# First block: two projection units and four gate units as seven block products each, the sums of their weights on GpSimd

## What is computed

```python
h = rms_norm(x, pre_norm_g[l])
u = jnp.einsum('bsd,de->bse', h, w_in[l])
u_mla, u_sb, u_moba, u_conv, u_gate = jnp.split(u, SPLITS, axis=-1)
...
qb, kb, vb = jnp.split(u_sb, 3, axis=-1)
o_b = merge_heads(stick_breaking_attention(split_heads(qb, H), ...))
qc, kc, vc = jnp.split(u_moba, 3, axis=-1)
o_c = merge_heads(moba_attention(split_heads(qc, H), split_heads(kc, H), split_heads(vc, H), rel_bias))
o_d = conformer_conv(u_conv, ...)
y = jnp.concatenate([o_a, o_b, o_c, o_d], axis=-1) * jax.nn.silu(u_gate)
y = jnp.einsum('bse,ed->bsd', y, w_out[l])
x = x + rms_norm(y, post_norm_g[l])
```

## Time and profile before

| what | us |
|---|---|
| median of 3 runs | 1030.85 |
| lowest, highest | 1030.44, 1031.91 |
| the profiled execution, own time | 1033.43 |
| its span (first to last instruction) | 1031.6 |
| PE busy | 998.9 (97%) |
| DVE busy | 720.6 (70%) |
| ACT busy | 202.0 (20%) |
| POOL busy | 77.2 (7%) |
| mean granted TensorE clock | 0.992 of full |

### The profile page before, as it was taken

One profiled execution on the slowest core, in us unless ns is written; L12 is line 12 of the kernel. 1 busy time (PEld: TensorE's weight loads), 2 busy tenths in 40 slices (PEclk: granted clock), 3 DMA queues, 4 the chain that ended last, 5 costly groups with the idle time before them and its releaser, 6 DMA issues. The chain is left out here.

```text
span 1031.6 us, 14106 instructions
## 1 busy us (share of the span) xinstructions
PE 998.9 (97%) x5350; PEld 728.8 (71%) x5352; DVE 720.6 (70%) x1683; ACT 202.0 (20%) x488; POOL 77.2 (7%) x89
## 2 busy tenths in 40 slices
PE   7999999999999999999999999989999999999994
PEld 4858764858865799757777777658996677777762
DVE  2695654695644587656899888985874677766668
ACT  4124323115222221202000000022222110010000
POOL 2000000000000000000002000062850000000000
PEclk9999999999999999999999999999999999999998
DMA  9854556655465546383679877824453345654411
GB/s 353 350 194 176 187 180 253 257 200 205 151 216 218 210 170 239 91 318 120 207 253 355 292 256 264 282 93 164 144 186 122 123 163 168 225 179 164 163 41 41
DMA packets 29914, 205.56 MB, mean 199 GB/s; under 512 B 3630, under 2 KB 3795, under 8 KB 6172
## 3 DMA queue, kind: packets, MB, share of 16 engines
q1 hardware_dynamic: 27116, 191.60, 51.6%
q0 software_dynamic: 2736, 13.11, 3.5%
HBM read 203.64 MB, written 1.05 MB: 198 GB/s over the span
## 5 line engine op out<-in xcount | busy, mean ns | idle before, releaser
L1650 PE MATMUL bank<-hT,raw 128*128 128x256 f32 x736 | 163.9, 383 | 2.1 <-DMA raw<-units_dram 2.1
L1650 PEld LDWEIGHTS bank<-hT,raw 128*128 128x128 f32 x736 | 140.0, 192 | 23.1 <-DMA raw<-units_dram 2.8
L1939 PE MATMUL bank<-yT,arena 128*128 128x512 f32 x224 | 100.8, 593 | 0.0
L1939 PE MATMUL bank<-raw,arena 128*128 128x512 f32 x180 | 86.8, 593 | 0.0
L1939 PEld LDWEIGHTS bank<-yT,arena 128*128 128x128 f32 x224 | 42.5, 190 | 53.8 <-issue 51.7
L876 DVE CUSTOM_DVE_ANT_0 raw<-raw,crow 128x1024 f32<-128x1024 f32 x64 | 75.4, 1220 | 0.5 <-DVEq L118 0.5
L1963 PEld LDWEIGHTS bank<-hT,raw 128*128 128x128 f32 x448 | 54.3, 192 | 12.4 <-issue 12.4
L726 ACT ACTIVATE arena<-bank 128x512 f32<-128x512 f32 x28 | 16.7, 597 | 197.0 <-PE bank L1963 197.0
L1963 PE MATMUL bank<-hT,raw 128*128 128x128 f32 x448 | 54.5, 275 | 0.0
L1660 PE MATMUL bank<-raw,yT 128*128 128x512 f32 x112 | 49.5, 596 | 0.9 <-DVE yT L1544 0.4
L909 DVE SCALAR_TENSOR_TENSOR arena<-arena 128x256 f32<-128x256 f32 x120 | 48.4, 481 | 0.1
(11 more groups left out here) (427 smaller groups left out, 1710.4 us busy)
## 6 DMA issues: line engine op xcount, KB each, us to landing
raw<-units_dram SPq DMA_DIRECT2D x180, 1024.0 KB, 4.9
arena<-ln_rows_dram POOLq DMA_DIRECT2D x4, 1024.0 KB, 5.1
arena<-att_line_dram POOLq DMA_DIRECT2D x4, 512.0 KB, 6.4
arena<-small_dram POOLq DMA_DIRECT2D x2, 896.0 KB, 7.5
arena<-ada_rows_dram POOLq DMA_DIRECT2D x1, 1536.0 KB, 8.0
xt<-x_dram SPq DMA_DIRECT2D x2, 512.0 KB, 4.6
arena<-post_g_dram POOLq DMA_DIRECT2D x2, 512.0 KB, 9.3
kst<-consts_dram SPq DMA_DIRECT2D x1, 608.0 KB, 16.4
```

What stands on the lines that cost most here:

```text
L1650: mm = pe.matmul(b[:, c * S:(c + 1) * S], raw[:, s, k * 256 + c * P:k * 256 + (c + 1) * P], act_t[:, k, :], start=(k == 0), stop=(k == KC ...
L1939: return pe.matmul(SB[i][:], x, y, start=False, stop=stop)
```

## The change

A unit is the product of a 1024 x 256 weight matrix with 1024 x 256 tokens. Cut in 2 x 2 blocks (128 columns by 512 rows of weights, 512 rows by 128 tokens) it takes eight block products; by the scheme of Winograd and Strassen it takes seven, of sums of blocks, and more sums behind them. A block product is 4 matmuls of 128x128 weights against 128 tokens, so a unit becomes 28 matmuls of 128 columns where it was 16 of 256.

- `first_part` on PE: the first part of a unit is four products (two of plain blocks, two of sums), the rest is three. For `U_CQ` and `U_CK` the parts go to different banks, in the old place. For a gate unit both go to G[1] one after the other: the rest is multiplied after the head's transposes, next scores and values, and waits for `half_drained`; the next unit's first part waits for `first_drained` of the one before. The transposes of the queries now wait for `first_drained` of `U_CQ`, whose banks they use.
- `first_weights` on POOL: four tensor-tensor operations of 128x512 for each unit, from `raw` into `gateT`, `yT` or the place of `mu`, as soon as the unit has landed and its target is free.
- `first_token_sums` on DVE: four of 128x512 for a layer, `hT` into `xs`, between `taps(0, 12)` and `ada_unit(3)`.
- `half_sums` and `rest_sums` on DVE: seven small operations for each unit, from PSUM to `part`, `qkC` or `gateT`.
- ACT no longer drains the two units; it scales `qkC[:, 0]` in place. The tanh reads `gateT` and stands behind the copies and exponentials of the pair, and the gate product on DVE stands behind the normalisation (`gate`), except for the last.

```diff
+            def first_weights(l, u):
+                n = FIRST[u]
...
+                wait_landed(pool, T1 * l, n)
+                if u == 2:
+                    pool.wait_ge(up_ready.sem, up_ready.at(l, 2))
+                    pool.wait_ge(rope_ready.sem, rope_ready.at(l, 2))
+                if u >= 3:
+                    wait_used(pool, T1 * l, FIRST[(1, 2, 4)[u - 3]])
+                ch.do(pool.tensor_tensor(d[:, 0], a[1][0], a[1][1], ALU.add))
+                ch.do(pool.tensor_tensor(d[:, 2], a[0][0], a[1][0], ALU.subtract))
+                ch.sync(1)
+                ch.do(pool.tensor_tensor(d[:, 1], d[:, 0], a[0][0], ALU.subtract))
+                ch.sync()
+                pool.tensor_tensor(d[:, 3], a[0][1], d[:, 1], ALU.subtract).then_inc(fsum_ready.sem, 1)
...
+            def half_sums(l, u, b):
+                p, o = b[:].rearrange("p (i n) -> p i n", i=4), FIRST_OUT[u]
+                dve.wait_ge(first_half.sem, first_half.at(l, u + 1))
+                ch.do(dve.tensor_copy(part[:, 2], p[:, 0]))
+                ch.sync()
+                ch.do(dve.tensor_tensor(o[0][:, 0], part[:, 2], p[:, 1], ALU.add))
+                ch.do(dve.tensor_tensor(part[:, 0], part[:, 2], p[:, 2], ALU.add))
+                ch.sync()
+                dve.tensor_tensor(part[:, 1], part[:, 0], p[:, 3], ALU.add).then_inc(half_drained.sem, 1)
+            def rest_sums(l, u, b):
...
+                wait_used(dve, T1 * l, FIRST[u])
+                dve.wait_ge(half_drained.sem, half_drained.at(l, u + 1))
+                ch.do(dve.tensor_tensor(part[:, 2], part[:, 0], p[:, 1], ALU.add))
+                ch.do(dve.tensor_tensor(o[1], part[:, 1:2].to_broadcast([P, NT, P]), p[:, 0:2], ALU.add))
+                ch.sync(1)
+                ch.do(dve.tensor_tensor(o[0][:, 1], part[:, 2], p[:, 2], ALU.add))
+                ch.sync()
+                dve.sem_inc(first_drained.sem, 1)
...
                 taps(0, 12)
+                first_token_sums(l)
                 ada_unit(l, 3)
...
+                half_sums(l, 0, A[2])
+                rest_sums(l, 0, A[3])
+                half_sums(l, 1, G[0])
+                rest_sums(l, 1, G[1])
                 ada_unit(l, 5)
...
                     if j % 2 == 0:
-                        gate(j // 2)
+                        half_sums(l, 2 + j // 2, G[1])
...
                         if j + 2 < 2 * H:
                             scores_max(j + 2)
+                            ada_unit(l, 6 + j // 2)
+                            rest_sums(l, 2 + j // 2, G[1])
                             scores_max(j + 3)
                             head_norm(8 * l, j + 2)
                             head_norm(8 * l, j + 3)
-                        ada_unit(l, 6 + j // 2)
+                            gate(j // 2)
+                        else:
+                            rest_sums(l, 2 + j // 2, G[1])
+                            gate(j // 2)
+                            ada_unit(l, 6 + j // 2)
...
-                unit_t(T1 * l, U_CQ, hT, G[0])
-                unit_t(T1 * l, U_CK, hT, G[1])
+                pe.wait_ge(upc_ready.sem, upc_ready.at(l, 6))
+                for u, b in ((0, A[2:4]), (1, G[0:2])):
+                    for rest in range(2):
+                        first_part(l, u, b[rest], rest)
...
+                pe.wait_ge(first_drained.sem, first_drained.at(l, 1))
...
                     if j % 2 == 0:
-                        if j >= 2:
-                            pe.wait_ge(silu_ready.sem, silu_ready.at(l, j // 2))
-                        unit_t(T1 * l, U_GATE[j // 2], hT, G[1])
+                        pe.wait_ge(first_drained.sem, first_drained.at(l, 2 + j // 2))
+                        first_part(l, 2 + j // 2, G[1], False)
```

More of the change, by code:

```diff
@@ L245, in build @@
         zT = zline[:, 2:4, :]
+        part = rt.rearrange("p a t h i -> p (a t h i)")[:, 0:3 * P].rearrange("p (i n) -> p i n", i=3)
         view2 = views()
@@ L390, in build @@
         msum_ready, mtsum_ready, mix_drained = (sem(n) for n in ("msum_ready", "mtsum_ready", "mix_drained"))
+        FIRST = (U_CQ, U_CK) + U_GATE
+        square4 = lambda b: b.rearrange("p (i k n) -> p i k n", i=4, k=4)
+        first_tsum, f_gate, f_y = (square4(b[:].rearrange("p a b -> p (a b)")) for b in (xs, gateT, yT))
+        at_mu = NCOL + NSMALL + D + H * S
+        f_mu = square4(arena[:, at_mu:at_mu + UNIT])
+        FIRST_SUMS = (f_gate, f_y, f_mu, f_y, f_mu, f_mu)
+        FIRST_OUT = [[qkC[:, i, c].rearrange("p (t n) -> p t n", t=NT) for c in range(2)] for i in range(2)]
+        FIRST_OUT += [[gateT[:, 2 * g + c].rearrange("p (t n) -> p t n", t=NT) for c in range(2)] for g in range(H)]
+        ftsum_ready, fsum_ready, first_half = event("ftsum_ready", 1), event("fsum_ready", 6), event("first_half", 6)
+        half_drained, first_drained = event("half_drained", 6), event("first_drained", 6)
         def wait_landed(eng, turns, n):
@@ L456, in _ @@
             pool.dma_start(wgk[0:17, :], gk_in).then_inc(gla_in, 16)
+            def first_weights(l, u):
+                n = FIRST[u]
+                w = raw[:, n % SLOTS, :].rearrange("p (k n) -> p k n", k=KC)
+                a = [[w[:, 4 * k:4 * k + 4, c * P:(c + 1) * P] for k in range(2)] for c in range(2)]
+                d = FIRST_SUMS[u]
+                wait_landed(pool, T1 * l, n)
[10 more added lines that the diff above has]
+                pool.tensor_tensor(d[:, 3], a[0][1], d[:, 1], ALU.subtract).then_inc(fsum_ready.sem, 1)
             pool.wait_ge(rr_ready, 1)
@@ L464, in _ @@
             pool.tensor_copy(moba_bias[:], zline[:, :, ::-1]).then_inc(bias_ready, 1)
+            for u in range(6):
+                first_weights(0, u)
             for l in range(1, DEPTH):
                 layer_vectors(l)
+                for u in range(6):
+                    first_weights(l, u)
             pool.wait_ge(x_new.sem, 2 * DEPTH + 2)
@@ L646, in _ @@
                 act.activation(spl[:], spl[:], ACT.Ln, bias=1.0).then_inc(spl_ready.sem, 1)
-                wait_used(act, T1 * l, U_CQ)
-                act.activation(qkC[:, 0], G[0][:], ACT.Copy, scale=HD_SCALE).then_inc(qk_ready.sem, 1)
-                wait_used(act, T1 * l, U_CK)
-                act.activation(qkC[:, 1], G[1][:], ACT.Copy).then_inc(qk_ready.sem, 1)
+                act.wait_ge(first_drained.sem, first_drained.at(l, 1))
+                act.activation(qkC[:, 0], qkC[:, 0], ACT.Copy, scale=HD_SCALE).then_inc(qk_ready.sem, 1)
                 for i, (dst, h0, b) in enumerate(((qT, 0, A[2]), (qT, 2, A[3]), (kT, 0, A[1]), (kT, 2, A[2]))):
@@ L660, in gate_tanhs @@
                 def gate_tanhs(g):
-                    wait_used(act, T1 * l, U_GATE[g])
+                    act.wait_ge(first_drained.sem, first_drained.at(l, 3 + g))
                     if g >= 1:
                         act.wait_ge(silu_ready.sem, silu_ready.at(l, g))
-                    act.activation(th[:].rearrange("p c s -> p (c s)"), G[1][:], ACT.Tanh, scale=0.5).then_inc(gate_tanh.sem, 1)
+                    act.activation(th[:], gateT[:, 2 * g:2 * g + 2, :], ACT.Tanh, scale=0.5).then_inc(gate_tanh.sem, 1)
                 def head_scale(j):
@@ L1730, in last_units, with first_part, product @@
                             mm.then_inc(o_ready.sem, 1)
+            def first_part(l, u, b, rest):
+                n = FIRST[u]
+                w = raw[:, n % SLOTS, :].rearrange("p (k n) -> p k n", k=KC)
+                a, ts = FIRST_SUMS[u], first_tsum
+                def product(i, x, y):
+                    for k in range(4):
+                        mm = pe.matmul(b[:, i * P:(i + 1) * P], x(k), y(k), start=k == 0, stop=k == 3)
+                    return mm
+                if not rest:
+                    wait_landed(pe, T1 * l, n)
+                    product(0, lambda k: w[:, k, 0:P], lambda k: hT[:, k, 0:P])
+                    product(1, lambda k: w[:, 4 + k, 0:P], lambda k: hT[:, 4 + k, 0:P])
+                    pe.wait_ge(ftsum_ready.sem, ftsum_ready.at(l, 1))
+                    pe.wait_ge(fsum_ready.sem, fsum_ready.at(l, u + 1))
+                    product(2, lambda k: a[:, 1, k], lambda k: ts[:, 1, k])
+                    product(3, lambda k: a[:, 2, k], lambda k: ts[:, 2, k]).then_inc(first_half.sem, 1)
+                else:
+                    if u >= 2:
+                        pe.wait_ge(half_drained.sem, half_drained.at(l, u + 1))
+                    product(0, lambda k: w[:, 4 + k, P:S], lambda k: ts[:, 3, k])
+                    product(1, lambda k: a[:, 0, k], lambda k: ts[:, 0, k])
+                    product(2, lambda k: a[:, 3, k], lambda k: hT[:, 4 + k, P:S]).then_inc(used[n % SLOTS], 1)
             pe.wait_ge(zeros_ready, 1)
@@ L1809, in _ @@
                 pe.wait_ge(qkT_ready.sem, qkT_ready.at(l, 4))
[L1810 removed]
+                pe.wait_ge(qk_ready.sem, qk_ready.at(l, 3))
+                pe.wait_ge(first_drained.sem, first_drained.at(l, 2))
                 def head_scores(j):
```

(2 more changed lines are left out.)

19 lines of the change are left out of this document (15 added, 4 removed).

## The result

The changed kernel takes 1069.98 us (median of 4 runs, 1068.35 to 1070.88) beside 1031.38 (4 runs, 1030.44 to 1032.23) on the same chip: a ratio of 1.0375 [1.0359, 1.0391], 38.6 us slower. The forecast was 1075.0. The profiled execution took 1070.88; its span is 1069.0 against 1031.6 before, 37.4 more.

A forecast was written before the change was run, and what follows sets the result against it. PE was taken to bound the kernel, with DVE's slack ahead of the logarithms as the limit. Layers of 21.4 and 19.2 us plus 3.5 of clock made 44.1, on 1030.85 the forecast 1075.0, own range 1066 to 1086.

The forecast's parts named there:

- What bounds it: PE busy 97% of the span; DVE has only 3.11 us of slack ahead of the logarithms (5.29 in layer 1).
- PE's saving, 0.70 a unit: Seven-product units take 6.25 us for 6.95; 12 units save 8.4 us, 4.2 in a layer.
- Token sums, 2.4 us in the slack: Ahead of the logarithms, four DVE token sums of 0.6 us each fit in the 3.11 us of slack.
- POOL and DVE take turns, taps included: Ahead of the logarithms, three units' sums cost DVE 5.0 us each; transposes 13.4 us late in layer 0, 11.2 in layer 1.
- taps are free: Rival: in the first block only token sums and ada products lose turns, not the taps; 1051 us, chance 0.09.
- The range's other end: In the taps, up to 0.3 us more per turn as DVE restarts its pipe; 12 turns a layer, +7 us.
- Waits of the loop: In the gate loop, new PE waits less 0.7 saved per unit: net +3.0, +1.3, +0.65, +3.1 for `U_G0` to `U_G3`.
- The clock, 1.7 a layer: Behind PE's idle ahead of the transposes, the lower clock costs 1.7 us per layer, between 0 and 3.5; +3.5 in all.
- The sum: Whole kernel: 21.4 us in layer 0, 19.2 in layer 1, 3.5 of clock, 44.1 us in all.
- No turns at all, 2.75 a layer: Rival: no turns in the first block, 2.75 us slower per layer, 5.5 in all; 1036.4 us, chance 0.11.

The follow-up runs named there:

- experiment 1: The changed kernel with POOL's four weight sums per unit replaced by fills with zero of the same tiles; 1038.65 us, ratio 1.0066.
- experiment 4: The changed kernel with one wait more: POOL begins the first gate unit's sums only when ACT's softplus is ready; 1063.31 us, ratio 1.0307.
- experiment 6: The changed kernel with PE's wait for the last gate moved from ahead of the first output unit to ahead of the second; 1062.95 us, ratio 1.0316.
- experiment 8: The changed kernel with only the last three gates in seven products, and POOL's sums and DVE's ada units placed elsewhere; 1040.86 us, ratio 1.0092.
- experiment 2: The changed kernel with query and key units whole again, drained by ACT, only the gates in seven products; 1047.69 us, ratio 1.0165.
- experiment 9: The kernel of experiment 8 with POOL's sums of the third and fourth gates at other times only; 1033.26 us, ratio 1.0023.
- experiment 10: The kernel of experiment 9 with POOL's sums replaced by fills with zero; 1031.41 us, ratio 0.9999.
- experiment 3: The changed kernel with the gates whole again in their old order, only query and key units in seven products; 1048.60 us, ratio 1.0161.
- experiment 5: The changed kernel with four more POOL additions and subtractions of the same form ahead of the first unit's sums; 1077.69 us, ratio 1.045.
- experiment 7: The changed kernel with DVE's half sums of the first gate moved ahead of its mask products; 1068.17 us, ratio 1.0354.
- experiment 11: The kernel of experiment 9 with the first gate's ada unit and the inverse root behind the second gate's half sums; 1035.67 us, ratio 1.0041.
- experiment 12: The kernel of experiment 11 with POOL's third and fourth gate sums earlier and the first gate's ada unit behind the second gate; 1030.94 us, ratio 0.9992.

## Why the prediction was right, and where its sizes were off

- **What bounds it.** Right. DVE's slack ahead of the logarithms was the limit, and it was overrun.
- **PE's saving, 0.70 a unit: too large.** From start to start, with the waits taken out, `U_CQ` takes 6.36 for 6.95, and the four gate units save 0.3 to 0.6 each, 1.7 together: 1.3 a layer less than the sum had. The 0.70 was read from another stage of the program, where nothing stands between the two parts of a unit.
- **Token sums, 2.4 us in the slack.** Right: 0.6 apart where POOL fills, and no delay (experiment 1).
- **POOL and DVE take turns, taps included.** Right, and the largest term. Its rival "taps are free" is refuted by the 0.62 us of a tap. Of each turn DVE lost 0.96, not 1.25: the token sum 0.95, the two ada products 1.9, the 16 taps 4.91 for five operations, the 22 taps 3.77 for four, in all 11.5 for 12 turns where 15.0 stood in the sum. This is the mis-sized term: the logarithms started at 91.58, not at 95.4, and the transposes were 10.0 late, not 13.4. The range's other end, up to 0.3 more at each turn because DVE restarts its pipe, is shown by no run: a turn cost less than the sum had, not more.
- **The Trainium skill** (SBUF — State Buffer, Who interferes with whom) lets a DVE operation with two SBUF inputs contend with a GpSimd operation that reads SBUF and not with one that only writes. The trace agrees on both: 0.62 us a tap in the mean with sums, 0.41 with fills.
- **Waits of the loop.** `U_G0` 0.59 and 1.64 for 1.7 and 2.0; `U_G2` 1.11 for 1.35; `U_G3` 1.40 for 2.0; ahead of `U_O0` 1.74 for 1.6: these places were right. At `U_G1` the forecast had 2.0 ahead of a first part, made by turns; what came is 0.52 ahead of the rest, for the half sums. The waits are 7.0 in all, for four units' 1.7 saved; the rest up to 5.8 lies in about 0.1 more at each wait. Forecast 8.0 net.
- **The clock, 1.7 a layer: too small.** 2.3 and 2.8 behind the transposes, 1.4 at a second fall in layer 1's loop, and 1.6 in the second network, which the sum didn't have: 8.1 for 3.5. The last two come and go between the profiles (experiments 4 and 6), so they belong to the execution as much as to the change.
- **The sum** 44.1 was 37.4: 3.4 less in each layer ahead of the transposes, 2.2 and 2.2 less in the loop without its clock, 4.6 more of clock, and 0.35 less by the earlier start. The mechanism and the order of the terms are right; that the total lies 5 us off and not 11 is partly luck, since the two errors have opposite signs. With its own clock term and the measured waits the sum would have given 1063.9, under the range of its own of 1066 to 1086.
- **No turns at all, 2.75 a layer.** The run with fills gives 3.4. PE's smaller saving is of the right sign and larger (1.3) than the difference; the other terms weren't separated.

## What to carry to other kernels

Before work is given to an idle engine, ask what its instructions share with the engine that has the least slack: here 12 GpSimd operations a layer took 11.5 us from VectorE at the one place where it had 3.1 to spare. Splitting a unit that hides other work is priced by what it hid, so list who used its full length. Take the saving of a rewrite from rows in the stage where it will stand.

## What the runs showed of the hardware

- A turn costs DVE about 0.96 us beside GpSimd's 1.27 us sums, and operations with a single tensor as input can pay it as well: 1.38 for 0.29 (128x128), 1.25 for 0.17 (128x2), rows of experiment 8. The size of DVE's operation hardly matters: both lose 1.1. A fill can be held too: in experiment 1 one at 75.65, beside DVE's 128x1024 operation with one tensor input (L929, 75.50 to 76.19), took 1.00 for 0.53.
- Who holds the other off depends on who comes first, for longer than one instruction. In experiment 4 a sum issued at 78.31 inside a run of 22 taps took 4.39 us, while the taps kept their 0.41 each; in the kernel after, where sums were already running when the taps began (61.79), each sum took its turn. The held sum isn't free for DVE: in experiments 2 and 4 the turns fell on the operations behind the taps (2.17 and 2.27 for 1.22). Only where those read PSUM or wait anyway, as in layer 1 of experiment 2, are fewer turns left. Why a sum gets in at one point and not at another isn't settled.
- How far the clock falls can't be told from the idle time alone. The first unit of the second network follows the same wait of 2.1 us in all kernels. The granted clock of the 4 us behind it is 1.00 in the kernel before and 0.59 in the kernel after. The unit took 7.38 us in the kernel before and in the profiles of experiments 4, 6, 9 and 10, but about 9.0 in the kernel after and in those of 1, 2, 3, 5, 7, 8, 11 and 12:
```profile
366.01 9.01 PE L2041 MATMUL bank<-hT,raw 128*128 128x128 f32 x64 [2.10 <-ACT hT L743]
```
What decides between the two isn't settled here; until it is, a difference of 1.6 us between two profiles says nothing by itself.
